# Repeated transposes in TensorE's two last waits, and the embedding factors of tiles 29 to 31 made in a group at gate slab 8

## What is computed

```python
u = rms_norm(h, norm_mix_w);  proj = u @ w_in          # two groups of heads
y = concat(hgrn2_heads(proj), gla_heads(proj)) @ w_out
h = h + y
e = rms_norm(p @ ple_proj, ple_norm_w)                 # "embedding"
gate = sigmoid(rms_norm(h, ple_gate_norm_w) @ ple_gate_w + ple_gate_b)
h = h + gate * e
out = rms_norm(h, final_norm_w)
```

## Time and profile before

| | |
|---|---|
| median of three runs | 2146.5 us |
| the profiled execution | 2146.18 us |
| its span | 2144.2 us |
| mean granted TensorE clock | 0.994 |
| TensorE matmul busy | 2121.2 us, 99% |
| VectorE busy | 1498.6 us, 70% |
| ScalarE busy | 1015.3 us, 47% |
| DMA, mean | 182 GB/s |

### The profile page before, as it was taken

The page is one execution under the profiler, slowest core; times in us unless marked ns, Lnnn a source line. Parts: engine busy times, 40 slices in busy tenths (PEclk is TensorE's granted clock), DMA queues, the critical chain, the costliest instruction groups (busy, mean ns, idle before and its releaser), DMA issues.

```text
span 2144.2 us, 29993 instructions
## 1 busy us (share of the span) xinstructions
PE 2121.2 (99%) x10076; PEld 1772.7 (83%) x10076; DVE 1498.6 (70%) x2955; ACT 1015.3 (47%) x1900; POOL 165.5 (8%) x244
## 2 busy tenths in 40 slices
PE   9999999999999999999999999999999999999996
PEld 8888888888888888888888888888888888888885
DVE  7577777776666677677767655566677777786788
ACT  7355555553443354544444443344455455443453
POOL 1001101110000000000101010000011100010110
PEclk9999999999999999999999999999999999999997
DMA  9525556654553454354535565344487685888876
GB/s 333 185 94 171 163 167 176 177 173 152 141 162 123 138 159 142 109 157 132 167 112 171 174 191 175 101 128 134 142 296 271 217 271 188 278 250 286 241 209 230
DMA packets 128634, 390.64 MB, mean 182 GB/s; under 512 B 14944, under 2 KB 17376, under 8 KB 127200
## 3 DMA queue, kind: packets, MB, share of 16 engines
q1 hardware_dynamic: 107104, 283.56, 38.3%
q0 software_dynamic: 21440, 105.92, 20.5%
HBM read 339.88 MB, written 139.72 MB: 224 GB/s over the span
## 4 chain that ended last, share of the span: by engine, by line
PE 94%; DVE 4%; issue 1%; ACT 0%; DMA 0%; DVEq 0%; SPq 0%
PE acc L947 24%; PE acc L949 24%; PE acc L948 24%; PE lv L1039 3%; PE ms L949 2%; PE tr L949 2%; PE tr L947 2%; PE ms L948 2%; PE tr L948 2%; PE ms L947 2%; PE so L1048 1%; PE so L1051 1%; PE so L1028 1%; DVE w_lo L1774 1%; DVE act_lo L1793 0%
## 5 line engine op out<-in xcount | busy, mean ns | idle before, releaser
L947 PE MATMUL acc<-act_hi,w_lo 128*128 128x512 f32 x2368 | 951.7, 402 | 0.8 <-DVE feat L2208 0.5
L949 PE MATMUL acc<-act_hi,w_hi 128*128 128x512 f32 x2368 | 923.8, 390 | 0.0
L948 PE MATMUL acc<-act_lo,w_hi 128*128 128x512 f32 x2368 | 922.8, 390 | 0.0
L1254 ACT CAST w_hi<-w_raw 128x1024 fp32r<-128x1024 f32 x339 | 343.7, 1048 | 450.3 <-PE acc L949 337.8
L949 PEld LDWEIGHTS acc<-act_hi,w_hi 128*128 128x128 f32 x2368 | 444.4, 188 | 94.5
L947 PEld LDWEIGHTS acc<-act_hi,w_lo 128*128 128x128 f32 x2368 | 445.6, 188 | 87.5 <-issue 3.0
L948 PEld LDWEIGHTS acc<-act_lo,w_hi 128*128 128x128 f32 x2368 | 445.8, 188 | 84.7 <-issue 1.2
L1774 DVE TENSOR_TENSOR w_lo<-w_raw,w_hi 128x1024 fp32r<-128x1024 f32 x339 | 402.5, 1221 | 112.8 <-ACT w_hi L1254 107.3
L1330 ACT ACTIVATE work<-work 128x512 f32<-128x512 f32 x120 | 75.4, 628 | 125.5 <-DVE work L1830 124.9
L1844 DVE COPY_PREDICATED work<-mask_sb,lv 128x256 f32<-128x256 uint8 x168 | 88.8, 529 | 7.5
L1268 ACT ACTIVATE work<-work 128x512 f32<-128x512 f32 x64 | 40.5, 632 | 94.5 <-DVE work L1810 94.5
(11 more groups left out here) (366 smaller groups left out, 2465.5 us busy)
## 6 DMA issues: line engine op xcount, KB each, us to landing
w_raw<-in_slabs SPq DMA_DIRECT2D x276, 512.0 KB, 4.5
w_sums<-in_slabs POOLq DMA_DIRECT2D x96, 512.0 KB, 5.8
w_raw<-w_sums SPq DMA_DIRECT2D x64, 512.0 KB, 4.9
w_sums<-w_sums POOLq DMA_DIRECT2D x32, 512.0 KB, 3.9
work<-e_scratch SPq DMA_DIRECT2D x56, 256.0 KB, 5.0
t_sums<-y_scratch POOLq DMA_DIRECT2D x24, 512.0 KB, 6.9
feat<-in_x_feat SPq DMA_DIRECT2D x8, 1024.0 KB, 11.9
e_scratch<-work SPq DMA_DIRECT2D x32, 256.0 KB, 5.8
```

What stands on the lines that cost most here:

```text
L947: nc.tensor.matmul(ps, lhs_lo, rhs_hi, start=start, stop=False)
L948: nc.tensor.matmul(ps, lhs_hi, rhs_lo, start=False, stop=False)
L949: return nc.tensor.matmul(ps, lhs_hi, rhs_hi, start=False, stop=stop)
L1254: nc.scalar.copy(w_hi[par][:, j, :], w_raw[j][:, :]).then_inc(w_hi_ready, 1)
```

## The change

1. The early groups begin at slab 8: eight groups of three, `MADE_EARLY` is all of tiles 8 to 31, `BY_DMA` stays tiles 8 to 27, and L2347 is no longer run for tiles 29, 30 and 31. `load_early(8)` uses the even set of buffers and waits for `g2_sum` of tiles 0 to 7. Groups 8, 9 and 10 are loaded as follows: 8 in slab 8, 9 and 10 in slab 9. Group 10 now waits for the stores of group 8 to land, since it uses the same buffers.
2. `busy(count)` repeats a transpose of one 128x128 block into the last token bank, whose content it writes anew: 16 times ahead of the wait for `z_sq` 2, and 15 times plus one between the row products and the wait for `diag_ready`. The signal `tok_ready` for the last quarter of the tokens comes with the last of these.

```diff
-        EARLY_AT = {n: range(HK + 3 * (n - 9), HK + 3 * (n - 9) + 3) for n in range(9, 16)}
+        EARLY_AT = {n: range(HK + 3 * (n - 8), HK + 3 * (n - 8) + 3) for n in range(8, 16)}
         MADE_EARLY = range(HK, HK + 3 * len(EARLY_AT))
-        BY_DMA = MADE_EARLY[:-1]
+        BY_DMA = MADE_EARLY[:-4]
...
                 if q == HK:
-                    sp.wait_ge(early_stored[0], HALVES * KT // 4 * 16 + 3 * 3 * 16)
+                    sp.wait_ge(early_stored[0], HALVES * KT // 4 * 16 + 4 * 3 * 16)
...
             def load_early(n):
 
-                turn = (n - 9) // 2
+                turn = (n - 8) // 2
+                if n == 8:
+                    sp.wait_ge(g2_sum, HK)
                 if n == 9:
                     sp.wait_ge(g2_ready, HK)
...
-                if n == 9:
+                if n in (8, 9):
                     load_early(n)
                 if n + 1 in EARLY_AT and n >= 9:
                     load_early(n + 1)
...
                     nc.tensor.matmul(z_rows[c], z_1[0][:, toks], ones[:, 0:1], start=False, stop=False)
+                busy(16)
                 pe.wait_ge(z_sq, 2)
                 for c in range(NC_):
                     last = nc.tensor.matmul(z_rows[c], z_1[1][:, c * C:(c + 1) * C], ones[:, 0:1], start=False, stop=True)
                 last.then_inc(rows_ready, 1)
+
+            def busy(count):
+
+                for _ in range(count):
+                    nc.tensor.transpose(tok_block(NC_ - 1)[:, 0:P], gate_at(1, TOKEN_FIRST)[:, (NC_ - 1) * C:NC_ * C], ident[:, :])
...
-                    last.then_inc(tok_ready, 1)
+                    if c < NC_ - 1:
+                        last.then_inc(tok_ready, 1)
...
             by_token()
             row_products()
+            busy(15)
+            nc.tensor.transpose(tok_block(NC_ - 1)[:, 0:P], gate_at(1, TOKEN_FIRST)[:, (NC_ - 1) * C:NC_ * C], ident[:, :]).then_inc(tok_ready, 1)
             factors()
...
             def early_embed(n):
 
-                vec_e.wait_ge(early_loaded[n % 2], HALVES * KT // 4 * 16 + ((n - 9) // 2 + 1) * 3 * 16)
+                vec_e.wait_ge(early_loaded[n % 2], HALVES * KT // 4 * 16 + ((n - 8) // 2 + 1) * 3 * 16)
```

## The result

| | before | changed |
|---|---|---|
| median | 2146.43 us (6 runs, 2144.7 to 2147.21) | 2155.14 us (6 runs, 2154.0 to 2157.41) |
| ratio | | 1.0044, 95% interval 1.0031 to 1.0056 |
| profiled execution, its span | 2146.18, 2144.2 us | 2155.04, 2153.0 us |

What follows compares the result with a forecast made beforehand. TensorE's matmuls bound the kernel up to the last gate matmul, then VectorE's lateness, TensorE's halved clock and the stores; 2146.18 - 2.1 (end) + 3.0 (stall) = 2147.1, plus 0.3 for the median: 2147.4 us, range 2144.0 to 2150.4.

Steps and rivals of the forecast that it cites:

- Part one: Kernel's end: dropping the multiplications of tiles 29, 30 and 31 makes VectorE's chain 1.9 us earlier.
- part two: Kernel's end: repeated transposes keep TensorE's clock full, four products take 0.94 us, VectorE goes on 2.1 us earlier.
- Rival 2: Kernel's end: transposes don't keep the clock, 0.3 us gained; 2149.2 with the stall (chance 0.27), 2146.2 without (0.1).
- eleven of the sixteen: Kernel's end, clock lost: eleven repeats through before the fall, five at 0.22 us each, VectorE 0.8 us earlier.
- Part three: Slabs 8 to 11: the added early group delays low weights and the next group's loads; costs 3.0 us.
- I take 1913.2: Slab 8: assumed landing of group 8's loads, from a median of 4.4 us, possible from 1911.2 to 1915.0.
- 1.4 to spare, no stall: Slab 10: low weights' first half done at 1917.9, TensorE needs it at 1919.35, so no wait.
- A stall of 3.0 us: Slab 11: TensorE waits for low weights done at 1933.2, needed at 1930.25; bounds from none to 5.2 us.
- the 1929.2 of the sum: Ahead of slab 11: VectorE begins group 9 at 1929.2, 7.4 us after its loads go out at 1921.8.
- Rival 3: SP's wait for group 8's stores before group 10's loads and slab 12's weights hands delay on; over 2150.8, chance 0.08.

Runs made afterwards that it cites:

- end_only: The kernel before with the repeated transposes alone, early groups as before; 2147.04 us, ratio 0.9997.
- rep10: first9 with ten repeated transposes in place of sixteen in the first wait, second lot kept; one execution, 25.9 us from last gate matmul to end of span.
- block8: The kernel before with VectorE held in slab 8 by 14 multiplications into an unused PSUM bank, no DMA added; one execution of 2153.77 us.
- first9: defer8 with SP issuing group 9's loads first thing in slab 9, ahead of group 8's stores; 2145.59 us against 2147.1, ratio 1.0.
- defer8: The changed kernel with VectorE multiplying group 8 in slab 9, behind slab 10's low weights, instead of in slab 8; 2150.06 us, ratio 1.0011.
- early_only: The changed kernel without the repeated transposes; 2156.34 us, ratio 1.0044.
- rep10_gap: rep10 with one of the last four scalings moved between z_variance and z_factor; 2144.5 us, ratio 0.999.

## Why the prediction was wrong

**Part one and part two** were right in what binds the end. Predicted -2.1 at the end, measured 28.48 - 26.17 = 2.3; `z_product(1)` on the heels of the last matmul, L1213's successor bound by the repeats, variance 6.45 us after the last matmul against 2122.3 - 2115.7 = 6.6. Rival 2 (the transposes don't keep the clock) did not come true: it stayed at 1.00 through the changed kernel's end, and in end_only it rose while only transposes ran. That is against the rule of the Trainium skill, page "TensorE: Matmul & The Clock Gate", section "Part 4: PE-mode transpose", that the full clock does not engage for a transpose; here the measurement decides. It does not follow that transposes hold the clock as well as matmuls do, since it fell in rep10 with no idle at all. But I also gave the repeats a part of the gain that they don't have. Without them the variance came after 6.1 us where the clock held, 0.3 sooner than with sixteen, and after 6.55 and 6.83 where it fell. So the number was right partly by luck: sixteen repeats cost as much in one execution as they save in another. (Rival 2's "eleven of the sixteen" are nine by the prediction's own start at 2119.6 and 0.11 each; that would have made its gain 0.4 us and not 0.8.)

**Part three** is the step that failed. It had the right chain (the blocked VectorE, the low weights, SP's queue, the next group), as block8 and first9 show, but four terms of its sum were wrong, all in one direction.
1. "I take 1913.2" for the landing of group 8. VectorE started on it at 1917.14, less 0.48 of later clock 1916.7: 3.5 late. I took the median landing; the slowest of the three loads landed 7.9 us after its issue, beyond the 6.2 of the earlier trace rows. A weight load issued sooner was late too: the second half of slab 10's raw weights, cast by 1910.6 before, waited for its DMA until 1912.3. Why they were late stays open. It is not the place on the queue: in the seven profiles whose kernels issue the same three loads at the same place, but let VectorE multiply them in slab 9 (defer8, first9 and those made from it), the slowest landed after 4.7 to 6.0 us. In early_only, which multiplies them in slab 8 like the changed kernel, it took 8.8. The six runs of the one kernel and the four of the other all took 2154.0 us or more, so it was hardly the chance of one execution.
2. "1.4 to spare, no stall" at slab 10: with 3.5 late it is a stall of 2.2, near the 2.1 that 3.5 - 1.4 gives.
3. "A stall of 3.0 us" at slab 11: 4.9. Group 9 went out at 1926.65, less 0.48 1926.2 (1921.8 expected: 3.5 us are the landing of group 8, the other 0.9 slower issuing) and took 8.9 instead of 7.4. So VectorE began group 9 at 1935.0, 5.8 us later than the 1929.2 of the sum, and 4.0 of them were given back because the first gap, with the half clock behind it, had already made TensorE late.
4. The clock was nowhere in the sum. A gap of 2.2 us was enough to halve it for over 3 us of full work; the two gaps cost 3.5 us beyond their length. I had used that price for the end and not for the stall.

2.2 + 4.9 + 3.5 = 10.6, less 2.3, and 0.5 from ahead of slab 8: 8.8 of span. The range went wrong by taking the bounds of the earlier trace rows for the landing, which these loads exceeded, by moving one term at a time, though a late landing of group 8 hands its delay to every later term, and by putting the clock behind a stall at nothing. Rival 3 named the handing on but put it a slab too late, at the stores of group 8 ahead of group 10; that wait was indeed long (SP took 6.76 us over the six loads) and cost nothing.

## What to carry to other kernels

A new load-and-use step in a covered stage must be given the same lead as its neighbours: here the groups from 10 on are loaded a slab ahead. Group 9 is not, and its wait was covered as long as it stood alone; a second group without a lead, right ahead of it, cost 10.6 us. The same work one slab later on VectorE, and with the loads ahead of the stores on SP, cost nothing. Where an engine's program order couples a wait to the next stage's operands, count the delay around the whole loop (load, wait, operands, the other queue's next load), and add the clock that a gap of the matmul engine takes away. Filling a wait with repeats helps only as long as they end before what is waited for, and whether the clock holds in such a stretch can't be told from one profile.

## What the runs showed of the hardware

- The granted clock rose from 0.50 to 1.00 while TensorE ran transposes and nothing else up to the last 0.2 us before the rise (end_only; and rep10, whose broadcast behind the slow repeats took 1.12 us, as at full clock).
- Transposes and 128x1 products without any idle between them did not always hold it: in rep10 it fell 6.0 us after the last 512-column matmul had begun, in rep10_gap, the same up to there, it did not.
- With 128x1 products and a wait of 1.1 us, the clock fell ahead of or among the last products in two of four profiles without repeats, and by then in none of six with ten or sixteen where the wait had been shortened; with the wait of 2.3 it fell in one of two in spite of sixteen.
- A stop of 2.2 us behind some 100 us of 512-column matmuls without one halved the clock when the matmuls began again (changed kernel, defer8, block8). block8's second gap of 1.47 us did not: the first matmul behind it took 0.47 us, the next 0.39 as always at full clock, and the windows behind it show 1.00.
- Without a gap, the stretch of nineteen gate slabs took 207.2 us in ten profiles of eight kernels, to 0.01 us.
